# Scores of a query tile against high and low keys in one matmul

## The chip, the cores and the metric

The kernel runs on one core of a Trainium2 chip. The metric is the device time of one execution in microseconds; lower is better. TensorE multiplies matrices into the eight banks of PSUM; VectorE, ScalarE and GpSimd work on what lies in the banks (the first two only) and in SBUF; SyncE issues the loads of the weights. The engines run side by side and wait for one another only through semaphores.

## The reference

Two layers of a small decoder over 256 positions of width 1024, each a residual around one input projection, a mixer and one output projection. What the change touches is the attention inside both mixers. The even layer has 8 heads of causal attention over the one block of 256 keys:

```python
l_own = jnp.einsum('bhqd,bhkd->bhqk', qc, k_own).astype(jnp.float32) * scale
l_own = jnp.where((kpos[None, :] <= qpos[:, None])[None, None], l_own, -jnp.inf)
p = jax.nn.softmax(jnp.concatenate([l_sel, l_own], axis=-1), axis=-1)
```

The odd layer has 16 heads, each with three windows of strides 1, 4 and 16, merged with weights in proportion to their denominators. With 256 positions this is one softmax over masked scores, with a key that lies in two or three windows counted so often; the kernel puts the logarithm of the count in the mask. So both layers need, for each head, scores = q k^T plus a mask, then the exponential, the sum and the product with the values.

## The kernel before, in words

Everything in float32 that goes through TensorE as a projection or as scores is split in two parts, high (rounded to a shorter format, fp32r) and low (what is left), and the product is the sum of high x high, high x low and low x high. Weights come by DMA into `w_raw`; ScalarE rounds them to `w_hi` (L631), VectorE subtracts to get `w_lo` (L780), and TensorE runs three matmuls a piece (L1011, L1013, L1015 with 256 columns; L1052 to L1054 with 512).

The work of all engines follows one list made by `steps()`: a hundred "product" items on TensorE, and between them, at places written out by hand (`HEADS_AT`, `EVEN_AT`, `NORM_AT` and so on), the steps of the heads. Each engine walks this list and does its own part of every step, so the order within an engine is fixed and waits are only on semaphores.

A head goes through four steps. "scores": TensorE writes q k^T to one of two banks (`score_banks[n % 2]`), VectorE adds the mask, scales and writes to `probs`, keeping the least value for each query (`least`), and ScalarE takes the exponential and its sum. "divide": VectorE. "transpose": TensorE turns `probs`, ScalarE copies to SBUF. "values": TensorE, for four heads at once.

The heads are worked in three sets of 8: set 0 the even layer's, sets 1 and 2 the odd layer's. For each head the queries stand as high and low parts stacked over the 128 rows (`q_stack`), and the high key stands twice (`k_twice`), so that one matmul gives (high + low of q) x high key. The low key (`k_low`) has zeros in the other half, so a second matmul adds high q x low key. Query tile 0 (positions 0 to 127) needs keys 0 to 127 only; tile 1 needs all 256. That is four matmuls a head: columns 0 to 127 of the bank twice (L1071, L1072), columns 128 to 383 twice. Columns 384 to 511 are not used.

VectorE's step (L924) is one instruction per query tile, of 128 and 256 columns, each followed by a read of its accumulator; the second signals `masked`. ScalarE waits for `masked` of the head, and TensorE's scores of head n wait for `masked` of head n - 2 (the bank). TensorE's transpose of head n waits for the division of head n (L932) and for ScalarE's copy of head n - 1. In the even layer VectorE also does the layer norm between the heads (L876 to L884), with a reciprocal root on GpSimd. `yT_lo` serves as the twice-written key in sets 0 and 1, and `k_own` in set 2.

Of the kernel before, what the change touches and what calls it, by code (L numbers as in the profile page):

```python
# [20 lines left out]
P = 128  # L21
SEQ = 256
# [224 lines left out]
def build(nc, x, x_turned, final_norm_g, ab_w_in, ab_w_out, gmlp_ln_g, gmlp_ln_b, gmlp_w_s, gmlp_b_s,  # L247
# [12 lines left out]
    with ctx:  # L260
# [3 lines left out]
        def sem(name):  # L264
            return ctx.enter_context(nc.semaphore(name))
# [8 lines left out]
        hnT_hi = sb("hnT_hi", [P, CHUNKS, SEQ], fp32r)  # L274
        hnT_lo = sb("hnT_lo", [P, CHUNKS, SEQ], fp32r)
        yT_hi = sb("yT_hi", [P, CHUNKS, SEQ], fp32r)
        yT_lo = sb("yT_lo", [P, CHUNKS, SEQ], fp32r)
        q_own = sb("q_own", [P, HEADS_OF_SET, SEQ], fp32r)
        k_own = sb("k_own", [P, HEADS_OF_SET, SEQ], fp32r)
        k_low = sb("k_low", [P, HEADS_OF_SET, SEQ], fp32r)  # L280
        v = sb("v", [P, TILES, D])
        gate = sb("gate", [P, 2, TILES, BLOCK])
        y = sb("y", [P, TILES, D])
# [18 lines left out]
        moments = sb("moments", [P, TILES, nc.vector.BN_STATS_DIM])  # L302
        meanvar = sb("meanvar", [P, TILES, nc.vector.BN_AGGR_DIM])

        ones = v[:, 0, 0:P]
        gain = gate[:, 0, :, :].rearrange("p a b -> p (a b)")
        xT = y[:].rearrange("p t c -> p (t c)").rearrange("p (k s) -> p k s", s=SEQ)
# [6 lines left out]

        q_stack = (yT_hi, yT_hi, q_own)
        k_twice = (yT_lo, yT_lo, k_own)

        ln_g, ln_b = gate[:, 0, 0, :], gate[:, 0, 1, :]

# [40 lines left out]
        added, scaled = sem("added"), sem("scaled")  # L360
        hidden_turned, hidden_hi, hidden_ready = sem("hidden_turned"), sem("hidden_hi"), sem("hidden_ready")
        scores_done, masked, probs_ready = sem("scores_done"), sem("masked"), sem("probs_ready")
        probs_turned, probsT_ready = sem("probs_turned"), sem("probsT_ready")
        values_done, inverted, attended = sem("values_done"), sem("inverted"), sem("attended")
        squared, inner_ready = sem("squared"), sem("inner_ready")
# [355 lines left out]
        def _(dve):  # L721
# [52 lines left out]
            for step in order:  # L774
# [98 lines left out]
                elif what == "layer_norm":  # L873
                    vt = hn[:, n, BLOCK:D]
                    dve.wait_ge(dve_emptied, dve_emptied_before(3) + 1)
                    chain(nc.vector.bn_stats(moments[:, n, :], vt), stats, n + 1)  # L876
                    nc.vector.bn_aggr(meanvar[:, n, :], moments[:, n, :]).then_inc(stats2, 1)
                    dve.wait_ge(stats2, n + 1)
                    dve.wait_ge(ln_loaded, 32)
                    nc.vector.scalar_tensor_tensor(out=vt, in0=vt, scalar=meanvar[:, n, 0:1], in1=ln_g,  # L880
                                                   op0=ALU.subtract, op1=ALU.mult).then_inc(centred, 1)
                    dve.wait_ge(centred, n + 1)
                    dve.wait_ge(ln_plus, 2 * n + 2)
                    nc.vector.scalar_tensor_tensor(out=vt, in0=vt, scalar=rstd[:, 6 + n:7 + n], in1=ln_b,  # L884
                                                   op0=ALU.mult, op1=ALU.add).then_inc(v_normed, 1)
                elif what == "mix_u":

                    dve.wait_ge(mix_done, n + 1)
                    dve.wait_ge(bias_loaded, 16)
                    dve.wait_ge(dve_emptied, dve_emptied_before(5) + 1)  # L890
                    for g in range(GROUPS):
                        cols = slice(g * P, (g + 1) * P)
                        last = nc.vector.scalar_tensor_tensor(
                            out=y[:, n, cols], in0=score_banks[n][:, cols], scalar=bias_s[:, g:g + 1],
                            in1=hn[:, n, cols], op0=ALU.add, op1=ALU.mult)
                    last.then_inc(mixed, 1)
                elif what == "gating":
                    for t in range(TILES):
                        if n == 1:

                            dve.wait_ge(mixed, TILES)
                            dve.wait_ge(dve_emptied, dve_emptied_before(6) + 1)
                            last = nc.vector.scalar_tensor_tensor(
                                out=y[:, t, 0:BLOCK], in0=y[:, t, 0:BLOCK], scalar=quarter_rstd2[:, t:t + 1],
                                in1=gate[:, 0, t, :], op0=ALU.mult, op1=ALU.mult)
                        else:
                            c = {0: 1, 2: 0, 3: 1}[n]
                            dve.wait_ge(attended, {0: EVEN_HEADS, 2: EVEN_HEADS + 8, 3: N_HEADS}[n] // BATCH)
                            dve.wait_ge(dve_emptied, dve_emptied_before({0: 4, 2: 15, 3: 16}[n]) + 1)
                            part = y[:, t, BLOCK:D] if n == 0 else y[:, c, t * BLOCK:(t + 1) * BLOCK]  # L910
                            last = nc.vector.tensor_tensor(part, part, gate[:, c, t, :], ALU.mult)
                    last.then_inc(gated, 1)
                elif what == "scores":

                    mask = mask_even if n < EVEN_HEADS else mask_odd
                    dve.wait_ge(scores_done, n + 1)
                    if n == 0:
                        dve.wait_ge(const_pool, 2)
                    if n == EVEN_HEADS:
                        dve.wait_ge(mask_built, 2)  # L920
                    if n >= 3:
                        dve.wait_ge(probs_turned, n - 2)
                    for t, (a, b) in enumerate(((0, P), (P, 3 * P))):
                        last = nc.vector.tensor_tensor_reduce(  # L924
                            out=probs[:, n % 3, a:b], in0=score_banks[n % 2][:, a:b], in1=mask[:, 2 * P - (b - a):],
                            scale=-SCALE, scalar=3e38, op0=ALU.add, op1=ALU.min, accum_out=least[:, n, t:t + 1])
                    last.then_inc(masked, 1)
                elif what == "divide":
                    dve.wait_ge(probs_ready, n + 1)
                    chain(nc.vector.reciprocal(den[:, n, :], den[:, n, :]), inverted, n + 1)  # L930
                    for t, (a, b) in enumerate(((0, P), (P, 3 * P))):
                        last = nc.vector.tensor_scalar(probs[:, n % 3, a:b], probs[:, n % 3, a:b], den[:, n, t:t + 1],  # L932
                                                       None, ALU.mult)
                    last.then_inc(probs_scaled, 1)
                elif what == "values":
                    dve.wait_ge(values_done, n + 1)
                    nc.vector.tensor_copy(turned_y(n), value_bank[:]).then_inc(attended, 1)
                elif what == "y_pair":
                    chunk, bank = y_place(n)
                    dve.wait_ge(y_hi, n + 1)  # L940
                    source = bank[:] if n in GMLP_PAIRS else turned_y(n if n < 2 else n - 2)
                    nc.vector.tensor_tensor(yT_lo[:, chunk:chunk + 2, :], source.rearrange("p (a b) -> p a b", b=SEQ),
                                            yT_hi[:, chunk:chunk + 2, :].bitcast(fp32), ALU.subtract).then_inc(y_lo, 1)
                elif what == "residual":
                    layer, t, c = n // TILES, n % TILES, step[2]
                    group = (7, 17)[layer] + t

                    dve.wait_ge(products_done, LAST_ITEM_OF_GROUP[group] + 1 - 2 * (1 - c))
                    cols = slice(c * BLOCK, (c + 1) * BLOCK)
                    nc.vector.tensor_tensor(h[:, t, cols], h[:, t, cols], pair(group)[c][:],  # L950
                                            ALU.add).then_inc(added, 1)
                elif what == "windows":
                    windows()
                elif what == "scale":
                    dve.wait_ge(added, 2 * n + 2)
                    scale_tile(2 + n, 2 if n < TILES else 1)
                elif what == "hidden":
                    hidden_low(n)

        @block.tensor  # L960
        def _(pe):
# [15 lines left out]
            for step in order:  # L977
# [79 lines left out]
                elif what == "scores":  # L1057
# [8 lines left out]
                        pe.wait_ge(masked, n - 1)  # L1066
                    q, k = q_stack[heads_set], k_twice[heads_set]
                    bank = score_banks[n % 2]
                    for t, (a, b) in enumerate(((0, P), (P, 3 * P))):
                        queries, keys = slice(t * P, (t + 1) * P), slice(0, b - a)  # L1070
                        nc.tensor.matmul(bank[:, a:b], q[:, i, queries], k[:, i, keys], start=True, stop=False)  # L1071
                        last = nc.tensor.matmul(bank[:, a:b], q[:, i, queries], k_low[:, i, keys],  # L1072
                                                start=False, stop=True)
                    last.then_inc(scores_done, 1)
                elif what == "transpose":
                    pe.wait_ge(probs_scaled, n + 1)
                    if n >= 1:
# [80 lines left out]
```

## Time and profile before

| | before |
|---|---|
| time, median of 3 runs | 264.58 us (264.01 to 265.3) |
| span of the profiled execution, first to last instruction | 261.6 us |
| TensorE matmul busy | 251.8 us, 96% |
| VectorE busy | 192.2 us, 73% |
| ScalarE busy | 159.2 us, 61% |
| GpSimd busy | 25.0 us, 10% |
| DMA | 44.59 MB, mean 170 GB/s |
| granted TensorE clock, mean | 0.997 of full speed |

The profiled execution's span is 3.0 us shorter than the median time; what lies around the span belongs to the execution but not to the program's instructions. A matmul's duration contains its way through the array, so matmuls overlap in the trace and their durations don't add up to time: the distance from one start to the next does. The same holds in part for VectorE, where an instruction often starts a little before the last one ends.

### The profile page before, as it was taken

The page shows a single profiled execution, that of the slowest core. Times are in us where ns is not written, and L with a number is a line of the kernel's source. Part 1 is how long each engine was busy: PE and PEld are TensorE (multiplying, and loading weights), DVE is VectorE, ACT ScalarE, POOL GpSimd, SP SyncE. Part 2 cuts the span into 40 slices and gives each one's busy share as a digit, 9 for nine tenths or more (in the row PEclk, how much of TensorE's full clock was granted, in tenths as well). Part 3 has the DMA queues.
Part 4 walks back from the last instruction along what each step waited for, and adds up shares of the span by engine and source line. Part 5 has one row for each costly group of instructions (what it writes and reads, how often), then busy time and mean ns, then how long its engine had stood idle before and what let it go on. Part 6 is the DMA issues. An engine that isn't in the chain of part 4 may idle for free.

```text
span 261.6 us, 4450 instructions
## 1 busy us (share of the span) xinstructions
PE 251.8 (96%) x1670; PEld 225.8 (86%) x1670; DVE 192.2 (73%) x383; ACT 159.2 (61%) x301; POOL 25.0 (10%) x52
## 2 busy tenths in 40 slices
PE   7999998999999999999999999999999999999990
PEld 6789997899888788887888999989999999987870
DVE  2977999988896999749577609396986779763643
ACT  5867776765737953746377646558688576550232
POOL 3007130001010000010200000210003000100021
PEclk9999999999999999999999999999999999999998
DMA  7999869350446466534638950827072440200004
GB/s 230 391 393 332 303 245 332 150 163 0 163 160 201 160 236 208 183 140 162 189 132 300 336 169 13 304 71 257 4 214 110 163 148 15 78 3 3 0 1 160
DMA packets 22452, 44.59 MB, mean 170 GB/s; under 512 B 1056, under 2 KB 1312, under 8 KB 22432
## 3 DMA queue, kind: packets, MB, share of 16 engines
q1 hardware_dynamic: 21712, 43.00, 47.8%
q10 hardware_dynamic: 576, 0.79, 0.9%
q0 software_dynamic: 144, 0.52, 0.6%
q8 instruction: 13, 0.21, 0.3%
q14 instruction: 7, 0.06, 0.1%
HBM read 43.26 MB, written 1.05 MB: 169 GB/s over the span
## 4 chain that ended last, share of the span: by engine, by line
PE 77%; DVE 9%; DMA 7%; issue 2%; ACT 2%; SPq 1%; POOLq 0%; POOL 0%; DVEq 0%
PE products L1052 12%; PE products L1054 12%; PE products L1053 12%; PE products L1011 10%; PE products L1015 10%; PE products L1013 10%; DMA w_raw<-in_ab_w_in 7%; DVE w_lo L780 4%; PE turned L963 4%; PE attended L1094 3%; DVE k_low L826 3%; PE scores L1071 2%; PE scores L1072 2%; DVE tanh L803 1%; ACT w_hi L631 1%
## 5 line engine op out<-in xcount | busy, mean ns | idle before, releaser
L780 DVE TENSOR_TENSOR w_lo<-w_raw,w_hi 128x1024 fp32r<-128x1024 f32 x74 | 88.9, 1226 | 7.3 <-ACT w_hi L631 6.6
L631 ACT CAST w_hi<-w_raw 128x1024 fp32r<-128x1024 f32 x74 | 75.6, 1047 | 26.3 <-PE products L1015 10.4
L1011 PE MATMUL products<-hnT_hi,w_hi 128*128 128x256 f32 x288 | 82.5, 286 | 0.3 <-DVE w_lo L780 0.3
L1015 PE MATMUL products<-hnT_hi,w_lo 128*128 128x256 f32 x288 | 81.5, 283 | 0.0
L1013 PE MATMUL products<-hnT_lo,w_hi 128*128 128x256 f32 x288 | 81.5, 283 | 0.0
L1011 PEld LDWEIGHTS products<-hnT_hi,w_hi 128*128 128x128 f32 x288 | 55.1, 191 | 0.9 <-DVE w_lo L780 0.7
L1013 PEld LDWEIGHTS products<-hnT_lo,w_hi 128*128 128x128 f32 x288 | 55.2, 192 | 0.0
L1015 PEld LDWEIGHTS products<-hnT_hi,w_lo 128*128 128x128 f32 x288 | 55.2, 192 | 0.0
L1052 PE MATMUL products<-w_hi,hnT_hi 128*128 128x512 f32 x80 | 31.9, 399 | 0.1
L687 ACT ACTIVATE probs<-probs,least 128x128 f32<-128x128 f32 (+1 forms) x48 | 21.4, 447 | 17.1 <-DVE least L924 17.1
L1054 PE MATMUL products<-w_lo,hnT_hi 128*128 128x512 f32 x80 | 31.2, 390 | 0.0
L1053 PE MATMUL products<-w_hi,hnT_lo 128*128 128x512 f32 x80 | 31.2, 390 | 0.0
L1052 PE MATMUL products<-w_hi,yT_hi 128*128 128x512 f32 x64 | 25.6, 400 | 0.0
L1053 PE MATMUL products<-w_hi,yT_lo 128*128 128x512 f32 x64 | 25.0, 390 | 0.0
L1054 PE MATMUL products<-w_lo,yT_hi 128*128 128x512 f32 x64 | 25.0, 390 | 0.0
L1052 PEld LDWEIGHTS products<-w_hi,hnT_hi 128*128 128x128 f32 x80 | 15.0, 188 | 3.4 <-issue 0.7
L1054 PEld LDWEIGHTS products<-w_lo,hnT_hi 128*128 128x128 f32 x80 | 15.0, 188 | 3.3
L1053 PEld LDWEIGHTS products<-w_hi,hnT_lo 128*128 128x128 f32 x80 | 15.1, 188 | 2.7
L1054 PEld LDWEIGHTS products<-w_lo,yT_hi 128*128 128x128 f32 x64 | 12.0, 188 | 2.6
L586 ACT ACTIVATE tanh<-h 128x512 f32<-128x512 f32 x8 | 5.1, 633 | 14.8 <-DVE h L950 14.7
L1052 PEld LDWEIGHTS products<-w_hi,yT_hi 128*128 128x128 f32 x64 | 12.0, 188 | 2.3 <-issue 0.2
L1053 PEld LDWEIGHTS products<-w_hi,yT_lo 128*128 128x128 f32 x64 | 12.0, 188 | 2.2
(152 smaller groups left out, 334.2 us busy)
## 6 DMA issues: line engine op xcount, KB each, us to landing
w_raw<-in_c_w_in SPq DMA_DIRECT2D x16, 1024.0 KB, 5.4
w_raw<-in_ab_w_in SPq DMA_DIRECT2D x12, 1024.0 KB, 6.1
w_raw<-in_ab_w_out SPq DMA_DIRECT2D x4, 1024.0 KB, 4.9
w_raw<-in_c_w_out SPq DMA_DIRECT2D x4, 1024.0 KB, 5.0
w_raw<-in_ab_w_in SPq DMA_DIRECT2D x4, 256.0 KB, 4.4
w_raw<-in_ab_w_in SPq DMA_DIRECT2D x2, 512.0 KB, 7.6
h<-in_x SPq DMA_DIRECT2D x2, 512.0 KB, 11.4
out<-hn SPq DMA_DIRECT2D x4, 256.0 KB, 2.2
```

Of the source, the lines that this page charges most:

```text
L631: nc.scalar.copy(w_hi[:, n % SPLIT_SLOTS, :, :], w_raw[:, half % RAW_SLOTS, part, :]).then_inc(hi_ready, 1)
L687: last = nc.scalar.activation(probs[:, n % 3, a:b], probs[:, n % 3, a:b], ACT.Exp, scale=-1.0, bias=least[:, n, t:t + 1], accum_out=den[:, ...
L780: nc.vector.tensor_tensor(w_lo[:, n % SPLIT_SLOTS, :, :], w_raw[:, half % RAW_SLOTS, part, :], w_hi[:, n % SPLIT_SLOTS, :, :].bitcast(fp32 ...
L826: last = nc.vector.tensor_tensor(to, bank[rows, :].rearrange("p (a b) -> p a b", b=SEQ), high.bitcast(fp32), ALU.subtract)
L963: return nc.tensor.matmul(to, of, ident[:], is_transpose=True, start=True, stop=True)
L1011: nc.tensor.matmul(to, wh, hi[:, chunk, :], start=begins and c % 2 == 0, stop=False, skip_group_check=True)
L1013: nc.tensor.matmul(to, wh, lo[:, chunk, :], start=False, stop=False, skip_group_check=True)
L1015: last = nc.tensor.matmul(to, wl, hi[:, chunk, :], start=False, stop=ends, skip_group_check=True)
L1052: nc.tensor.matmul(to[:], xh, w_hi[:, slot, half_item, :], start=begins, stop=False)
L1053: nc.tensor.matmul(to[:], xl, w_hi[:, slot, half_item, :], start=False, stop=False)
L1054: last = nc.tensor.matmul(to[:], xh, w_lo[:, slot, half_item, :], start=False, stop=ends)
L1094: last = nc.tensor.matmul(value_bank[rows_of(a), two * SEQ:(two + 1) * SEQ][:, queries], v[:, tile, column:column + HEAD], turned_probs(he ...
```

## The change

For query tile 0 one matmul of 256 columns takes the place of two of 128. Its moving operand is the high keys 0 to 127 and the low keys 0 to 127 of the head, which lie in neighbouring blocks of one tensor, `k_parts`, that takes the place of `yT_lo`, `k_low` and `k_own`. Its results go to the first and the last 128 columns of the bank and aren't summed there. VectorE first adds the last 128 columns and the mask into `probs`, then masks tile 1, waits for its own addition (`low_masked`) and masks tile 0 with the sum in the mask's place. Tile 1 on TensorE is as before. In sets 0 and 1 the high part goes to the front of the bank and the low one to the end, in set 2 the other way round.

```diff
-        yT_lo = sb("yT_lo", [P, CHUNKS, SEQ], fp32r)
         q_own = sb("q_own", [P, HEADS_OF_SET, SEQ], fp32r)
-        k_own = sb("k_own", [P, HEADS_OF_SET, SEQ], fp32r)
-        k_low = sb("k_low", [P, HEADS_OF_SET, SEQ], fp32r)
+        k_parts = sb("k_parts", [P, 3, HEADS_OF_SET, SEQ], fp32r)
...
+        yT_lo, k_low, k_own = (k_parts[:, i, :, :] for i in range(3))
...
+        k_both = (k_parts[:, 0:2, :, :], k_parts[:, 0:2, :, :], k_parts[:, 1:3, :, :])
...
-                    for t, (a, b) in enumerate(((0, P), (P, 3 * P))):
+                    bank = score_banks[n % 2]
+                    own_low = probs[:, n % 3, 0:P]
+                    nc.vector.tensor_tensor(own_low, bank[:, 3 * P:], mask[:, P:], ALU.add).then_inc(low_masked, 1)
+                    for t, (a, b) in ((1, (P, 3 * P)), (0, (0, P))):
+                        if t == 0:
+                            dve.wait_ge(low_masked, n + 1)
                         last = nc.vector.tensor_tensor_reduce(
-                            out=probs[:, n % 3, a:b], in0=score_banks[n % 2][:, a:b], in1=mask[:, 2 * P - (b - a):],
+                            out=probs[:, n % 3, a:b], in0=bank[:, a:b], in1=mask[:] if t else own_low,
                             scale=-SCALE, scalar=3e38, op0=ALU.add, op1=ALU.min, accum_out=least[:, n, t:t + 1])
                     last.then_inc(masked, 1)
...
-                    for t, (a, b) in enumerate(((0, P), (P, 3 * P))):
-                        queries, keys = slice(t * P, (t + 1) * P), slice(0, b - a)
-                        nc.tensor.matmul(bank[:, a:b], q[:, i, queries], k[:, i, keys], start=True, stop=False)
-                        last = nc.tensor.matmul(bank[:, a:b], q[:, i, queries], k_low[:, i, keys],
-                                                start=False, stop=True)
-                    last.then_inc(scores_done, 1)
+
+                    apart = bank[:].rearrange("p (a b) -> p a b", b=P)[:, 0:4:3, :]
+                    nc.tensor.matmul(apart, q[:, i, 0:P], k_both[heads_set][:, :, i, 0:P], start=True, stop=True)
+                    nc.tensor.matmul(bank[:, P:3 * P], q[:, i, P:SEQ], k[:, i, :], start=True, stop=False)
+                    nc.tensor.matmul(bank[:, P:3 * P], q[:, i, P:SEQ], k_low[:, i, :], start=False,
+                                     stop=True).then_inc(scores_done, 1)
```

## Rows read from the trace of the kernel before

**Rows 1.** The page: span, part 1 (busy) and part 4 (chain that ended last).

```profile
span 261.6 us, 4450 instructions
PE 251.8 (96%) x1670; PEld 225.8 (86%) x1670; DVE 192.2 (73%) x383; ACT 159.2 (61%) x301; POOL 25.0 (10%) x52
PE 77%; DVE 9%; DMA 7%; issue 2%; ACT 2%; SPq 1%; POOLq 0%; POOL 0%; DVEq 0%
```

**Rows 2.** TensorE's waits: releaser, us in total, times, longest us.

```profile
PE scores L1071 <- DVE least L924: 0.6, 1, 0.6
PE products L1011 <- DVE w_lo L780: 0.3, 1, 0.3
```

**Rows 3.** Busy time by stretch: length, each engine's busy us, clock, DMA share, GB/s.

```profile
171.00:233.00 62.00, 61.41 (x516) 58.93 (x516) 50.34 (x145) 42.32 (x104) 3.29 (x6) 1.00 0.34 111
```

**Rows 4.** TensorE's timeline around head 2: start us, duration us, line, operation, form.

```profile
47.60 0.39 PE L1054 MATMUL products<-w_lo,hnT_hi 128*128 128x512 f32 x1
47.82 0.22 PE L1071 MATMUL scores<-yT_lo,yT_hi 128*128 128x128 f32 x1
...
48.28 0.40 PE L1052 MATMUL products<-w_hi,hnT_hi 128*128 128x512 f32 x1
```

**Rows 5.** Timeline of the weight loads of head 12.

```profile
186.37 0.19 PEld L1071 LDWEIGHTS scores<-yT_lo,yT_hi 128*128 128x128 f32 x1
186.48 0.19 PEld L1072 LDWEIGHTS scores<-k_low,yT_hi 128*128 128x128 f32 x1
186.59 0.19 PEld L1071 LDWEIGHTS scores<-yT_lo,yT_hi 128*128 128x128 f32 x1
186.70 0.19 PEld L1072 LDWEIGHTS scores<-k_low,yT_hi 128*128 128x128 f32 x1
186.82 0.19 PEld L1011 LDWEIGHTS products<-hnT_hi,w_hi 128*128 128x128 f32 x1
```

**Rows 6.** TensorE's timeline: products of 256 columns, two in a row.

```profile
175.20 0.28 PE L1015 MATMUL products<-hnT_hi,w_lo 128*128 128x256 f32 x1
175.32 0.28 PE L1011 MATMUL products<-hnT_hi,w_hi 128*128 128x256 f32 x1
```

**Rows 7.** Groups by line and form: busy us, mean ns of one, idle before.

```profile
L924 DVE CUSTOM_DVE_ANT_0 probs<-scores,mask_odd 128x128 f32<-128x128 f32 x16 | 4.6, 286 | 0.8 <-PE scores L1072 0.7
L768 DVE SCALAR_TENSOR_TENSOR hnT_lo<-scores,gain_of,hnT_hi 128x128 fp32r<-128x128 f32 x8 | 2.2, 343 | 0.6 <-ACT hnT_hi L595 0.6
```

**Rows 8.** VectorE's timeline: the query splits and mask 0.

```profile
43.93 2.80 DVE L826 TENSOR_TENSOR yT_hi<-tanh,yT_hi 64x512 fp32r<-64x512 f32 x4
46.76 0.29 DVE L924 CUSTOM_DVE_ANT_0 probs<-scores,mask_even 128x128 f32<-128x128 f32 x1
...
46.98 0.42 DVE L924 CUSTOM_DVE_ANT_0 probs<-scores,mask_even 128x256 f32<-128x256 f32 x1
47.32 0.08 DVE L924 DVE_READ_ACCUMULATOR2_ANT least<- 128x1 f32 x1
```

**Rows 9.** TensorE's timeline: the transpose of head 3.

```profile
63.79 0.49 PE L963 MATMUL turned<-ident,probs 128*128 128x128 f32 x3
```

**Rows 10.** VectorE's timeline: mask 3, and the division of head 3.

```profile
58.30 0.29 DVE L924 CUSTOM_DVE_ANT_0 probs<-scores,mask_even 128x128 f32<-128x128 f32 x1 [0.41 <-PE scores L1072]
...
62.77 0.55 DVE L932 TENSOR_SCALAR probs<-probs,den 128x128 f32<-128x128 f32 x2
```

**Rows 11.** VectorE's timeline: the weight splits ahead of mask 8, and its end.

```profile
171.32 2.36 DVE L780 TENSOR_TENSOR w_lo<-w_raw,w_hi 128x1024 fp32r<-128x1024 f32 x2
...
174.27 0.08 DVE L924 DVE_READ_ACCUMULATOR2_ANT least<- 128x1 f32 x1
```

**Rows 12.** TensorE's timeline: the scores of head 10.

```profile
174.41 0.33 PE L1071 MATMUL scores<-yT_lo,yT_hi 128*128 128x128 f32 x1 [0.58 <-DVE least L924]
```

**Rows 13.** VectorE's timeline: the division of head 13.

```profile
194.96 0.55 DVE L932 TENSOR_SCALAR probs<-probs,den 128x128 f32<-128x128 f32 x2
```

**Rows 14.** TensorE's timeline: the transpose of head 13.

```profile
196.33 0.49 PE L963 MATMUL turned<-ident,probs 128*128 128x128 f32 x3
```

More of the change, by code:

```diff
@@ L362, in build @@
         scores_done, masked, probs_ready = sem("scores_done"), sem("masked"), sem("probs_ready")
+        low_masked = sem("low_masked")
         probs_turned, probsT_ready = sem("probs_turned"), sem("probsT_ready")
```

## The prediction

> **What bounds the kernel now.** I read the page first. TensorE is busy 96% of the span and carries 77% of the chain that ended last, VectorE 9% of it [rows 1]. A busy TensorE is not yet a bound, so the waits of TensorE come next: in the whole run it stands still on VectorE's score work for 0.6 us, in one place, and on the low halves of the weights for 0.3 us [rows 2]. The rest is matmuls back to back. So a microsecond taken from TensorE's stream comes off the span, unless VectorE is then late; and VectorE work costs nothing except at those places where TensorE reaches a wait soon after VectorE has signalled. VectorE has room on average: in the stretch with the odd layer's heads it is busy 50.34 of 62.00 us [rows 3]. The question is therefore local: what a head's matmuls cost, and where a later mask is felt.
>
> **What a head costs TensorE, and what is saved.** A head is four matmuls, each with its own weight load: 128 columns high and low for query tile 0, 256 columns high and low for tile 1. Start to start from the first of them to the next product, head 2 takes 48.28 - 47.82 = 0.46 us [rows 4]. The weight loads show why: they start 0.11, 0.11, 0.11 and 0.12 us apart, whatever the width of the matmul behind them [rows 5]. A matmul of 128 columns thus takes a turn of 0.11 us, one of 256 columns 0.12 us, which the products of 256 columns confirm (0.12 us from one to the next, each with a load) [rows 6]. The change leaves three matmuls of 256 columns: 3 x 0.12 = 0.36 us. It saves 0.46 - 0.36 = 0.10 us a head, 24 x 0.10 = 2.4 us in all. The number of columns stays 768 a head, so this gain exists only because a turn is bounded by its load and not by its columns.
>
> The new matmul reads its moving operand in two pieces of 128 columns, 2048 elements apart (8 heads x 256: high and low keys lie in neighbouring blocks of one tensor), and writes 128 columns at either end of a bank. The trace has no matmul of this form. Below, it can't beat a load's turn, 0.11 us; above, I bound it by a product of 512 columns, 0.22 to 0.23 us (47.60 to 47.82) [rows 4]. I take 0.12, the row of the same width, as the columns, the partitions and the bank are the same.
>
> A rule speaks against the change. The Trainium skill (TensorE: Matmul & The Clock Gate, "Back-to-back issue gap") gives an isolated gap of N/2.4 + 2.5 ns; by that a head would be about 330 ns before and 328 ns after, and the change would save nothing. The measured 0.46 us a head disagrees with it here. A rival below has the same outcome, worked out from rows.
>
> **What VectorE gets.** Each head gains one addition of 128 x 128 from a bank and SBUF to SBUF, and the two masks swap places. The mask of 128 columns lasts 286 ns [rows 7] and that of 256 columns 0.42 us [rows 8], but the next instruction starts before it ends: 46.76 to 46.98 is 0.22 us for the first, 46.98 to 47.32 is 0.34 us for the second [rows 8]. The addition isn't in the trace. Nearest are the mask of the same shape (0.22 us to the next) and the scaled subtraction of 128 x 128 from a bank, 343 ns long (some 0.27 us to the next if it overlaps as the masks do) [rows 7]. I take 0.21 to 0.22 us: like the mask it has no pointer operand. The floor is the time of its 128 elements by the difference of the two masks, about 0.13 us; the ceiling the whole 0.34 us. The wait for the addition's own semaphore (low_masked) is set in front of the last mask, with a mask of 0.34 us between; the semaphore has long risen, so I cost the wait at nothing, and at up to 0.04 us if that cover were gone. Behind it on VectorE stand the next splits and divisions, and ScalarE's exponentials wait for the same masked signal. Total 24 x 0.21 = 5 us of VectorE.
>
> The Trainium skill (VectorE: DVE Perf Modes, "The DRAIN you can't avoid") says that the next instruction doesn't start until the pipe is empty, by which an addition would hold VectorE for its full length. The starts above contradict it by 0.08 us; by the page the four additions that I charge below would cost 0.3 us more.
>
> SBUF gets the same bytes under another name, the GpSimd clearing and key copies work on the same elements, no DMA is added or moved, and no queue is passed. Those cost nothing.
>
> **Where the addition reaches the path.** I went through every wait of TensorE on a mask, on a division (the transposes) and on ScalarE's copy, and compared it with the end of what it waits for. Three are tight.
>
> *Scores of head 2* wait for mask 0. VectorE comes to mask 0 when its query splits end (43.93 + 2.80 = 46.73) [rows 8], not when the scores do, so mask 0 ends 0.21 us later: 47.40 becomes 47.61. TensorE comes at 47.82 - 2 x 0.10 = 47.62, but its weight load, which carries the wait, wants to go about 0.1 us ahead. So of the 0.20 us gained about 0.15 is lost, and 0.05 stays; with head 2 itself the lead is 0.15.
>
> *Transpose of head 3*, at 63.79 [rows 9]. Its division ends at 62.77 + 0.55 = 63.32 [rows 10], 0.47 us before. That division comes out of a chain which starts when the scores of head 3 are done: mask 3 at 58.30, mask 4, the layer norm's statistics, a trip over GpSimd, and the division [rows 10]. Two additions are now inside it, 0.42 us, while its start comes 0.15 + 0.10 = 0.25 earlier. The division ends at 63.32 + 0.42 - 0.25 = 63.49 and TensorE can go at about 63.65 (signal and load, as above). TensorE's lead there is 0.14 us, in place of the 0.55 (7 x 0.10 - 0.15) that heads 0 to 6 would give: 0.4 us lost. With head 7 the lead is 0.24 at the end of the even set. Up to head 8 all further work, the norm and the splits of the keys, is led by TensorE and keeps this lead.
>
> *Scores of head 10* wait for mask 8; this is the 0.6 us wait [rows 2]. VectorE is in one run from the key splits over two weight splits (171.32 + 2.36 = 173.68) to mask 8, whose last part ends at 174.35, and TensorE starts at 174.41 [rows 11, 12]. Here 0.21 us of addition goes straight on the path, and what heads 8 and 9 save turns into longer waiting. Lead: 0.24 - 0.21 = 0.03.
>
> From head 10 on, heads 10 to 23 save 14 x 0.10 = 1.4 us. The tightest division left with a mask ahead of it is that of head 13, which ends at 194.96 + 0.55 = 195.51, 0.8 us before its transpose at 196.33 [rows 13, 14]; additions and TensorE's lead together take at most 0.5 us of that. The division of head 16 is tighter still, but follows a copy of TensorE's own output with no mask between, so it keeps step. The low halves of weights are several microseconds ahead (how seldom they are waited for: [rows 2]).
>
> **Sum:** 0.03 + 1.4 = 1.43, and some 0.05 more for turns of 0.113 and not 0.11: 1.5 us. The profiled execution is 261.6 us from first to last instruction, and 3.0 us lie around it up to the median of 264.58; the change doesn't touch those. 264.58 - 1.5 = 263.1 us.
>
> **The rivals.**
> (a) *TensorE's time goes by columns, and the change doesn't do what it says.* No gain; mask 8 adds 0.21, and transpose 3 about 0.1: 264.9 us. Against it: at the rate of the 512-column product (0.23 us) 768 columns would take 0.34 us, and a head takes 0.46. 0.07.
> (b) *The two-piece matmul is slow.* One mechanism, at L1071's replacement: the additions alone cost about 0.3 us (mask 8 and the transpose of head 3, as in (a)), which heads 10 to 23 earn with 0.02 us each, so it decides from 0.12 + 0.08 = 0.20 us on; at the bound of 0.23 us a head takes 0.47 us, 24 x 0.01 = 0.2 us are lost instead of saved, and with the additions' 0.3 us the time is 265.1 us, slower than before. For it: no row shows the form. Against it: a stride within a partition's row is nothing that the low and high halves don't have already. 0.10.
> (c) *The additions hold VectorE for 0.34 us.* Then four of them on the path cost 0.13 us more each, 0.5 us: 263.6 us. For it: the length of the scaled subtraction. 0.15.
> (d) *The additions hide.* VectorE's order lets mask 0 and the division of head 3 come in time, and only mask 8 counts: 22 x 0.10 - 0.21 = 2.0 us, or 2.4 us if not even that: 262.4 us. Against it: the three tight places. 0.15.
> The forecast has the remaining 0.53.
>
> **Numbers.** Predicted 263.1. Low end: case (d) with the turns at 0.113, 262.2. High end: between (c) and (a), with the spread of the runs shown (264.01 to 265.3), 264.4. Leaving out (a), (b) and the lowest part of (d) leaves out two in ten. A measurement of this kernel can tell 0.5% from no change, that is 1.3 us: 263.26 is the border, and the forecast lies just beyond it. Faster: most of (d) and two thirds of the forecast, 0.5. Slower by over 0.5% needs 265.9, which (b) reaches only if the matmul is worse than its bound: 0.05. The rest, 0.45, within.
>
> **What the profile after would show.** A head of 0.36 us start to start; three loads; the addition at 0.29 us with the next instruction 0.21 us after its start; a wait for mask 8 grown from 0.6 to about 1.0 us; a short wait of TensorE at the transpose of head 3; and the last product 1.4 to 1.5 us earlier. What would make it wrong: a two-piece matmul that isn't 0.12 us, an addition of over 0.3 us to the next, or a fourth tight place that VectorE's shifted queue makes.

## The result, and the profile after

The changed kernel takes 261.82 us (median of six executions, 261.52 to 262.04), the kernel before 264.29 us (median of six beside it, 263.68 to 265.56). The ratio is 0.9915, 95% interval 0.9891 to 0.9939: faster by 0.85%, between 0.61% and 1.09%. The forecast was 263.1 us with a range from 262.2 to 264.4: the direction was right, and the time lies 0.4 us below the range.

The page of the changed kernel: span, busy time and, after the dots, the chain that ended last.

```profile
span 260.3 us, 4426 instructions
PE 249.4 (96%) x1646; PEld 223.3 (86%) x1646; DVE 196.4 (75%) x407; ACT 158.9 (61%) x301; POOL 25.0 (10%) x52
...
PE 75%; DVE 11%; DMA 7%; issue 2%; ACT 2%; SPq 1%; POOL 1%; POOLq 0%; DVEq 0%
```

Beside [rows 1]: TensorE has 24 instructions less and VectorE 24 more, one for each head. VectorE's share of the chain grew from 9 to 11%. A span also holds the first loads, whose arrival differs between executions, so I compare the part behind them: from the first scores matmul to the last product. In the kernel before these two stand at 45.46 and 254.72, 209.26 us apart; in the changed one they are these, 207.68 us apart.

```profile
45.78 0.36 PE L1078 MATMUL scores<-k_parts,yT_hi 128*128 128x256 f32 x1 [1.10 <-DVE yT_hi L828]
...
253.46 0.39 PE L1061 MATMUL products<-w_lo,yT_hi 128*128 128x512 f32 x1
```

That is 1.58 us less, where the sum was 1.4 to 1.5. Below, "the stream" is the same stretch up to the start of the third matmul from the end, where the last half item of products begins. It is 208.80 us in the kernel before (208.81 in a second trace of it, below) and 207.23 us in the changed one: 1.57 us less. Each of the two kernels has two traces; in these it repeats to 0.01 and 0.07 us, where whole times of one kernel differ by up to 2 us. One profiled execution below, that of the semaphore alone, took 418.87 us at a granted clock of 0.56 and gives no stream.

Head 1 on TensorE's timeline (start us, duration us, line, operation, form):

```profile
46.21 0.28 PE L1078 MATMUL scores<-k_parts,yT_hi 128*128 128x256 f32 x1
46.33 0.28 PE L1079 MATMUL scores<-k_parts,yT_hi 128*128 128x256 f32 x1
46.45 0.28 PE L1080 MATMUL scores<-k_parts,yT_hi 128*128 128x256 f32 x1
46.56 0.40 PE L1059 MATMUL products<-w_hi,hnT_hi 128*128 128x512 f32 x1
```

From first matmul to next product a head takes 46.56 - 46.21 = 0.35 us, where head 2 took 0.46 [rows 4]. The first of the three is the matmul with the moving operand in two pieces and its result at both ends of the bank; its turn is 0.12 us like that of the others. The weight loads of head 12 say the same, beside [rows 5]:

```profile
186.34 0.19 PEld L1078 LDWEIGHTS scores<-k_parts,yT_hi 128*128 128x128 f32 x1
186.45 0.19 PEld L1079 LDWEIGHTS scores<-k_parts,yT_hi 128*128 128x128 f32 x1
186.57 0.19 PEld L1080 LDWEIGHTS scores<-k_parts,yT_hi 128*128 128x128 f32 x1
186.69 0.19 PEld L1018 LDWEIGHTS products<-hnT_hi,w_hi 128*128 128x128 f32 x1
```

VectorE's timeline at mask 0, beside [rows 8]. The first row is the addition: 0.20 us to the next instruction. The last mask, which waits for low_masked, starts 0.34 us after the mask of 256 columns, and 0.34 us is also what follows that mask in the kernel before, where nothing waits (46.98 to 47.32).

```profile
47.08 0.30 DVE L927 TENSOR_TENSOR probs<-scores,mask_even 128x128 f32<-128x128 f32 x1
47.28 0.42 DVE L931 CUSTOM_DVE_ANT_0 probs<-scores,mask_even 128x256 f32<-128x256 f32 x1
47.62 0.08 DVE L931 DVE_READ_ACCUMULATOR2_ANT least<- 128x1 f32 x1
47.62 0.29 DVE L931 CUSTOM_DVE_ANT_0 probs<-scores,probs 128x128 f32<-128x128 f32 x1
```

The stretch with the odd layer's heads, beside [rows 3]: VectorE is busy 53.33 us in place of 50.34, with 162 instructions in place of 145.

```profile
171.00:233.00 62.00, 61.01 (x507) 58.24 (x506) 53.33 (x162) 43.09 (x107) 3.26 (x6) 1.00 0.34 111
```

The three tight places. TensorE's wait for mask 8, at the scores of head 10 (releaser, us in total, times, longest), beside [rows 2]:

```profile
PE scores L1078 <- DVE least L931: 1.0, 1, 1.0
```

It is 1.0 us in place of 0.6. The two others are short gaps on the timeline, at the scores of head 2 and the transpose of head 3:

```profile
47.72 0.39 PE L1061 MATMUL products<-w_lo,hnT_hi 128*128 128x512 f32 x1
47.98 0.39 PE L1078 MATMUL scores<-k_parts,yT_hi 128*128 128x256 f32 x1
48.20 0.28 PE L1079 MATMUL scores<-k_parts,yT_hi 128*128 128x256 f32 x1
...
63.44 0.28 PE L1022 MATMUL products<-hnT_hi,w_lo 128*128 128x256 f32 x1
63.84 0.55 PE L970 MATMUL turned<-ident,probs 128*128 128x128 f32 x3
```

At head 2 the first matmul starts 0.26 us behind a product of 512 columns, where it was 0.22 [rows 4], and its own turn is 0.22 in place of 0.12: from product to scores 0.04 us is lost, and in the head 0.10, so the 0.10 that this head should save is gone and 0.04 more. At head 3 the transpose starts 0.40 us after a product whose turn is 0.12 us: 0.28 us lost. The rows of the weight loads at the two places name what they waited for, mask 0 and the division of head 3:

```profile
47.98 0.19 PEld L1078 LDWEIGHTS scores<-k_parts,yT_hi 128*128 128x128 f32 x1 [0.29 <-DVE least L931]
...
63.84 0.31 PEld L970 LDWEIGHTS turned<-ident,probs 128*128 128x128 f32 x3 [0.33 <-DVE probs L939]
```

### The profile page after: what moved, and what is told of

It is laid out like the page before. It is cut to its first block, busy times and chain, and to the rows that moved or that the text cites. A ratio compares the mean times of both kernels' runs of the same rounds, so it can differ in the third digit from the quotient of the medians.

```text
span 260.3 us, 4426 instructions
## 1 busy us (share of the span) xinstructions
PE 249.4 (96%) x1646; PEld 223.3 (86%) x1646; DVE 196.4 (75%) x407; ACT 158.9 (61%) x301; POOL 25.0 (10%) x52
## 4 chain that ended last, share of the span: by engine, by line
PE 75%; DVE 11%; DMA 7%; issue 2%; ACT 2%; SPq 1%; POOL 1%; POOLq 0%; DVEq 0%
PE products L1059 12%; PE products L1061 12%; PE products L1060 12%; PE products L1018 9%; PE products L1022 9%; PE products L1020 9%; DMA w_raw<-in_ab_w_in 7%; DVE w_lo L782 5%; PE turned L970 4%; PE attended L1101 3%; DVE k_parts L828 3%; PE scores L1078 1%; DVE tanh L805 1%; PE scores L1080 1%; PE scores L1079 1%
## 5 line engine op out<-in xcount | busy, mean ns | idle before, releaser
L1060 PE MATMUL products<-w_hi,k_parts 128*128 128x512 f32 x64 | 25.0, 390 | 0.0
L538 POOL CAST k_parts<-k_parts 64x512 fp32r<-64x512 f32 x12 | 8.5, 706 | 77.8 <-ACT k_parts L645 77.2
```

The source lines that it names most:

```text
L538: nc.gpsimd.tensor_copy(to[rows_of(1 - side), heads_of(i, side), :], to[rows_of(side), heads_of(i, side), :].bitcast(fp32)).then_inc(keys_ ...
L1060: nc.tensor.matmul(to[:], xl, w_hi[:, slot, half_item, :], start=False, stop=False)
```

## The experiments

Each ratio is against executions of the kernel before on the same chip, with its 95% interval. The times of several single edits can't be told from no change, so the reading goes by the stream of the profiled execution, and by the time less its own span, which each execution gives. The diffs of the addition alone, the matmul alone, the four heads and the two tight places are against the changed kernel, the last one against the version with the eased places, the others against the kernel before; "..." marks what is left out.

**The kernel before, unchanged.** Its edit is empty.

> The kernel before, unchanged. Two theories of why the change measured 2.5 us (0.85%) where the two profiled executions differ by 1.3 us (261.6 and 260.3): (A) the profiled execution of before was a quick one of a kernel whose executions spread, and the change's true worth is what TensorE's stream shows, 1.3 to 1.5 us, plus something that the slower executions of before lose at a place where the new kernel doesn't; then the spans here spread from 261.6 to over 263 us with 1.7 us around each, as in the new kernel, and the slow ones lose it in the first 45 us, where the loads of the weights set the pace. (B) before has 3.0 us around its span and the executions are alike; then the spans here lie within 0.5 us of 261.6.

263.77 us, ratio 1.0009 (0.9991 to 1.0027), beside 29 executions with a median of 263.70 (263.38 to 265.59). The stream is 208.81. Two findings. The time less the span is 2.01 to 2.10 us in all twelve, not 3.0. And the times bunch: 36 of these 41 between 263.4 and 264.1, five between 264.7 and 265.6. The profiled one took 264.67 us, span 262.6, and shows where such time goes. The third piece of x on which ScalarE works waits for its load:

```profile
8.70 0.51 ACT L604 ACTIVATE hnT_hi<-y,hn 128x256 fp32r<-128x256 f32 x1 [2.17 <-DMA y<-in_x_turned]
```

In the first trace of the same kernel the row of the same piece is this, without a wait:

```profile
6.72 0.51 ACT L604 ACTIVATE hnT_hi<-y,hn 128x256 fp32r<-128x256 f32 x1
```

The stream behind it is equal to 0.01 us. So the difference between these two arises before it, and the late load of x is what the trace shows there. Two other traces below are of long executions too: 262.92 us in the matmul alone (median 261.50) and 263.22 us in the four heads (median 261.92). In these ScalarE waits 0.75 and 0.82 us for its first piece of x, where the other traces have 0 to 0.6, and the first scores matmul starts at 46.95 and 47.24, against 46.50 in the one above and 45.30 to 46.07 in the traces of shorter executions. For the long executions without a trace the same cause is likely and not shown.

**The tensor alone.** `k_parts` in place of the three, all the rest as before.

> Only the three tensors yT_lo, k_low and k_own are put into k_parts; matmuls and masks as before. If the other addresses in SBUF are worth something (theory C), this is 0.5 to 1 us faster than before; by A and B it is the same, ratio within 0.2% of 1.

```diff
-        yT_lo = sb("yT_lo", [P, CHUNKS, SEQ], fp32r)
-        k_own = sb("k_own", [P, HEADS_OF_SET, SEQ], fp32r)
-        k_low = sb("k_low", [P, HEADS_OF_SET, SEQ], fp32r)
+        k_parts = sb("k_parts", [P, 3, HEADS_OF_SET, SEQ], fp32r)
...
+        yT_lo, k_low, k_own = (k_parts[:, i, :, :] for i in range(3))
```

263.79 us, 1.0003 (0.9987 to 1.0019), stream 208.82. The place of the keys costs nothing.

**The addition alone.** Four matmuls, the low one of tile 0 to the end of the bank; VectorE as in the changed kernel.

> Four matmuls as before, but the low one of tile 0 goes to the end of the bank, and VectorE adds and masks as in the new kernel. By the account of the tight places: mask 0 has 0.4 us of room, the division of head 3 0.4 and mask 8 none, so 0.2 us at mask 8 and up to 0.1 at the transpose of head 3: 0.2 to 0.4 us slower than before (0.1%). If the additions weigh more than I think (0.34 us each): 0.5 to 0.8 us slower.

```diff
-                    nc.tensor.matmul(apart, q[:, i, 0:P], k_both[heads_set][:, :, i, 0:P], start=True, stop=True)
+                    nc.tensor.matmul(bank[:, 0:P], q[:, i, 0:P], k[:, i, 0:P], start=True, stop=True)
+                    nc.tensor.matmul(bank[:, 3 * P:], q[:, i, 0:P], k_low[:, i, 0:P], start=True, stop=True)
```

263.71 us, 0.9992 (0.9975 to 1.0008), stream 209.07: 0.27 longer than before. Its wait for mask 8:

```profile
PE scores L1078 <- DVE least L931: 0.8, 1, 0.8
```

0.6 became 0.8: with TensorE's number of matmuls unchanged, 24 additions cost little more than one. From the scores of head 9 to those of head 10 it is 1.41 us (173.33 to 174.74) in place of 1.21 (173.20 to 174.41), which is 0.20 for the addition. The whole time did not follow the stream: the time less the span is 1.69 to 1.84 us here, against 2.01 to 2.10 in the kernel before.

**The matmul alone.** One matmul of 256 columns, no addition, VectorE as before. This kernel leaves the low keys out of tile 0's scores, so it computes something else and serves only for its time.

> The one matmul of 256 columns, without the addition: the low keys of tile 0 are left out of its scores, VectorE works as before. TensorE saves 24 x 0.10 = 2.4 us, less what heads 8 and 9 save (0.2) and a part of heads 0 and 1: 2.1 to 2.3 us against before by the stream, span near 259.4. If the measured gain of the new kernel holds 1 us of something else (theory C), 3.2 us.

```diff
-                    nc.vector.tensor_tensor(own_low, bank[:, 3 * P:], mask[:, P:], ALU.add).then_inc(low_masked, 1)
-                    for t, (a, b) in ((1, (P, 3 * P)), (0, (0, P))):
-                        if t == 0:
-                            dve.wait_ge(low_masked, n + 1)
+                    for t, (a, b) in enumerate(((0, P), (P, 3 * P))):
...
-                            out=probs[:, n % 3, a:b], in0=bank[:, a:b], in1=mask[:] if t else own_low,
+                            out=probs[:, n % 3, a:b], in0=bank[:, a:b], in1=mask[:, 2 * P - (b - a):],
```

261.50 us, 0.9905 (0.9875 to 0.9935), stream 206.61: 2.19 us less than before. The time less the span is 2.02 to 2.09, as in the kernel before. Its wait for mask 8:

```profile
PE scores L1075 <- DVE least L928: 0.8, 1, 0.8
```

Two heads of saving, 0.2 us, went into that wait, and the other 22 x 0.10 = 2.2 arrive. The two parts alone give -2.19 + 0.27 = -1.92, together they give -1.57. The remaining 0.35 us is their meeting: once TensorE is ahead, additions are felt that weren't at TensorE's old pace. Which ones, the experiment with four heads below tells.

**The changed kernel again.**

> The changed kernel, unchanged, beside the same runs of before as the next three. The executions of before fall in two groups, most near 263.7 us and some near 265.3 us, by how the first loads arrive, so that three or six of them give an uneven median. If the true gain is the stream's (span 261.6 to 260.1, 1.5 us) and 0.35 us around the span (2.07 before, 1.72 in the changed kernel), the two medians differ by 1.9 us, ratio 0.993. If the first measurement of 2.5 us holds, 0.9905.

262.01 us (261.76 to 263.20), 0.9935 (0.9913 to 0.9957), beside seventeen executions of the kernel before with a median of 263.74. Stream 207.30, time less span 1.67 to 1.76. Against this even sample of the kernel before, the change brings 263.74 - 262.01 = 1.7 us, 0.65%.

**Four heads in the old form.** Heads 0, 3, 4 and 8, whose additions I had charged, keep four matmuls and two masks.

> Heads 0, 3, 4 and 8, whose additions lie on the path by my account, are done as before (two matmuls of 128 columns, no addition), the other twenty as in the change. By the account: TensorE saves 19 x 0.10 (head 9's goes into the wait for mask 8), the wait for mask 8 is 0.2 us shorter than in the changed kernel and that at the transpose of head 3 goes: span 1.9 us under before, 0.3 to 0.4 us under the changed kernel. If additions cost by their number on VectorE and not by their place: TensorE loses 0.4 us, VectorE gains little, and it is 0 to 0.4 us slower than the changed kernel.

```diff
+AS_BEFORE = (0, 3, 4, 8)
...
+                    if n in AS_BEFORE:
+                        nc.tensor.matmul(bank[:, 0:P], q[:, i, 0:P], k[:, i, 0:P], start=True, stop=False)
+                        nc.tensor.matmul(bank[:, 0:P], q[:, i, 0:P], k_low[:, i, 0:P], start=False, stop=True)
+                    else:
+                        nc.tensor.matmul(apart, q[:, i, 0:P], k_both[heads_set][:, :, i, 0:P], start=True, stop=True)
```

261.92 us (261.24 to 263.22), 0.9927 (0.9902 to 0.9953). The times can't be told from those of the changed kernel; the stream can: 206.88, 0.35 less than 207.23. Its wait for mask 8:

```profile
PE scores L1085 <- DVE least L934: 0.7, 1, 0.7
```

Four heads gave back 0.1 us each of saving and the stream still became shorter. So these four additions cost 0.65 to 0.75 us between them (0.65 if head 8's saving is taken to go into the wait for mask 8 in any case, as in the matmul alone). The other twenty cost at most 0.2: their heads save 20 x 0.105 = 2.1 us, 0.2 more than the 1.92 measured.

**Two tight places eased by the order.** The changed kernel, with the transpose of head 3 and the scores of head 10 each one half item of products later in the order written out by hand.

> The changed kernel with two places moved: the scores of head 10 one half item later (behind a product, 1.44 us), and the transpose of head 3 one later. Then mask 8 (ends 174.5) is there before TensorE comes (174.9), and the division of head 3 too. By the account this takes off the waits of 1.15 and 0.3 us, and mask 9 may then be late by 0.1 to 0.3 for the scores of head 11: 1.1 to 1.4 us faster than the changed kernel, span near 258.9. If the waits come back in full elsewhere: the same as the changed kernel.

```diff
-     (6, 8, 10, 13, 18, 19, 21, 23),
+     (6, 8, 10, 14, 18, 19, 21, 23),
...
-     (3, 4, 4, 6, 11, 13, 13, 14)),
+     (3, 4, 5, 6, 11, 13, 13, 14)),
```

260.99 us (260.63 to 262.35), 0.9897 (0.9873 to 0.9921), stream 206.21, 1.02 us less than the changed kernel's. The wait for mask 8 is gone from TensorE's waits. This is the fastest of the kernels tried. The largest gap that remains is further on, at the transpose of head 8 and the scores of head 11, which now meet mask 9:

```profile
176.49 0.28 PE L1022 MATMUL products<-hnT_hi,w_lo 128*128 128x256 f32 x1
176.61 0.49 PE L970 MATMUL turned<-ident,probs 128*128 128x128 f32 x3
177.08 0.39 PE L1078 MATMUL scores<-k_parts,yT_hi 128*128 128x256 f32 x1
```

From transpose to scores it is 0.47 us, where head 12 needs 0.25 in the changed kernel (186.12 to 186.37): 0.2 us lost.

**The same places in the kernel before.** The two lines of the last diff, in the kernel before.

> The kernel before with the same two places. Its wait for mask 8 is 0.75 us and it has none at the transpose of head 3, so 0.6 to 0.75 us faster than before. The difference of e7 and this is then the change freed of the places where its additions are felt: 24 x 0.10 = 2.4 us, less at most 0.3.

263.03 us, 0.9975 (0.996 to 0.999), stream 207.96, 0.84 less than before; time less span 2.01 to 2.12. So most of the gain from the order is there without the change. With the order eased in both, the change is worth 207.96 - 206.21 = 1.75 us of stream and 263.03 - 260.99 = 2.0 us of time (0.33 of it around the span). I had expected 2.1 to 2.4 of stream: a miss. The gap at mask 9, 0.2 us, the scores of head 2, some 0.1, and a gap of 0.17 us ahead of the transpose of head 10 (184.94 to 185.23, where the turn is 0.12) make up most of the difference from 2.4.

**The semaphore alone.** In the kernel before, the first mask of each head also signals `low_masked`, for which nobody waits.

> The kernel before; the first mask of each head also signals low_masked, which nobody waits for. The time around the span is 2.0 to 2.1 us in before and in every kernel without the additions, and 1.7 to 1.8 us in every kernel with them. If one more semaphore in use makes the difference, it is 1.7 us here; if it goes by VectorE's number of instructions, 2.0 to 2.1 us. Span as before, 261.6 us.

```diff
+                        if t == 0:
+                            last.then_inc(low_masked, 1)
...
```

263.80 us, 1.0003 (0.9979 to 1.0026), time less span 2.01 to 2.11: as the kernel before. Neither the semaphore nor its signals move what lies around the span.

**Twenty-four more instructions on VectorE.** In the kernel before, one addition of one column a head, into a column of the bank that nothing reads.

> The kernel before with one more tiny VectorE instruction a head (one column, into a column of the bank that nobody reads) and no new semaphore. If the number of instructions makes the difference around the span, 1.7 to 1.8 us here; if the semaphore, 2.0 to 2.1 us. The span may grow by some 0.1 us, since the instruction stands ahead of mask 8.

```diff
+                    nc.vector.tensor_tensor(score_banks[n % 2][:, 3 * P:3 * P + 1], mask[:, 0:1], mask[:, 1:2], ALU.add)
```

263.46 us, 0.9988 (0.9975 to 1.0001), which as a whole time isn't clear of no change. The time less the span is 1.68 to 1.76 us, as in the changed kernel. Part 3 of the page (packets, MB, share) shows one thing that goes with it, here

```profile
q14 instruction: 8, 0.07, 0.1%
```

and in the kernel before

```profile
q14 instruction: 7, 0.06, 0.1%
```

The kernels with 7 packets (before, the tensor alone, the matmul alone, the places in the kernel before, the semaphore alone) have 2.01 to 2.12 us around the span, those with 8 (changed, the addition alone, the four heads, this one, the last one below) 1.67 to 1.84. The version with the eased places has 9 packets and 1.70 to 1.75, so one packet more changes nothing further. What the kernels of the second group have in common is 20 to 24 instructions more on VectorE, and an addition of one column does as well as one of 128. TensorE's number doesn't matter: the matmul alone has 24 less and 2.02 to 2.09. Why a longer program on VectorE should end or begin in less time outside the span, no run here shows.

**The places, head 0 in the old form, head 11 later.** From the version with the eased places.

> The changed kernel with the two places of e7, the scores of head 11 also one half item later (in e7 they wait some 0.2 us for mask 9), and head 0 done as before, so that mask 0 isn't late for the scores of head 2. By the account of the tight places: 0.2 to 0.4 us off e7 in the span from the first scores to the last product (206.2 us in e7): 205.8 to 206.0 us, and 1.1 to 1.4 us under the changed kernel. If moving a wait only moves it on, 206.2 us or more.

```diff
-     (3, 4, 5, 6, 11, 13, 13, 14)),
+     (3, 4, 5, 7, 11, 13, 13, 14)),
...
+AS_BEFORE = (0,)
...
```

261.40 us (261.30 to 262.94), 0.9927 (0.9908 to 0.9946), stream 206.95: 0.74 us worse than the version it came from, where 0.2 to 0.4 better was expected. ScalarE's timeline, then TensorE's:

```profile
180.46 0.40 ACT L690 ACTIVATE probs<-probs,least 128x128 f32<-128x128 f32 x1 [0.65 <-DVE least L934]
...
181.35 2.36 ACT L646 CAST q_own<-products 64x512 fp32r<-64x512 f32 x4
...
184.81 0.48 ACT L698 COPY probsT<-turned 128x384 f32<-128x384 f32 x1
```

```profile
185.43 0.52 PE L973 MATMUL turned<-ident,probs 128*128 128x128 f32 x3 [1.02 <-ACT probsT L698]
```

The exponential of head 11 comes later and ScalarE stands at it for its mask; behind it in ScalarE's order are the split of the queries and the copy of the turned `probs`, and TensorE waits 1.02 us for that copy at the transpose of head 10. The step that I moved had room on TensorE and on VectorE, and none on ScalarE. The two traces also show how far the expectation held. Counted from the first scores matmul, TensorE is 0.02 us ahead of the version with the eased places at the scores of head 8, so head 0 in the old form gives back about what it gains, and 0.26 us ahead at the transpose of head 9, so the later scores of head 11 did bring some 0.24. At the transpose of head 10 it is 0.75 us behind.

## Why the prediction was right or wrong

**What a head saves: right.** 0.35 us a head in place of 0.46. By the matmuls of head 1 the saving is 0.11 us, by the weight loads of head 12 it is 0.10; 24 x 0.105 = 2.5 us. Rival (a), time by columns, is out: the 768 columns of a head are what they were, and the head is a quarter shorter. By the formula in the Trainium skill (TensorE: Matmul & The Clock Gate, "Back-to-back issue gap") the estimate is 328 ns for the new head and 330 for the old; it comes near the 0.35 of three wide matmuls and misses the 0.46 with narrow ones, whose loads start 0.11 us apart. But the section itself calls this the gap of an isolated matmul and says that for narrow ones in a stream with weight loads it counts too little, so the prediction was wrong to call it a rule against the change.

**The two-piece matmul: right.** Taken at 0.12 from the row of the same width; it is 0.12. Rival (b) is out.

**The addition: right.** Taken at 0.21 to 0.22 to the next instruction, 0.20 to 0.21 measured, with a length of 285 ns at its line. The next instruction starts 0.08 us before it ends. The prediction took from the Trainium skill (VectorE: DVE Perf Modes, "The DRAIN you can't avoid") that it would wait for the end. The same section adds that a next instruction which isn't held starts earlier, and with that the trace agrees. The wait for `low_masked` costs nothing. Rival (c), 0.34 us, is out.

**The tight places: right, with small errors.** The wait for mask 8 went from 0.6 to 1.0 us, as forecast. The transpose of head 3 waits. The lead of TensorE lost there is 0.28 us, where I had 0.4; the loss at the scores of head 2 is 0.14, where I had 0.15. The wait for mask 8 is 0.4 longer. Together 0.82 us, of 2.5 - 1.57 = 0.95 that is lost of the heads' saving. Of the 0.4 at mask 8, 0.2 is the saving of heads 8 and 9, which goes into that wait without any addition too (the matmul alone). The other 0.6 is the additions', and the four heads in the old form show that it is nearly all due to the four that I had charged. Rival (d), in which the additions hide, is out, though the time came out near its 262.4. The time alone would have pointed to the wrong mechanism.

**The sum of the stream: right.** -1.43 to -1.5 forecast, -1.57 in one trace and -1.50 in another.

**The step that failed** is the one that turns the stream into a time: "The profiled execution is 261.6 us from first to last instruction, and 3.0 us lie around it up to the median of 264.58; the change doesn't touch those." Both halves are wrong. The 3.0 was the span of one execution taken from the median of others. In every execution of this kernel where span and time are both known 2.0 to 2.1 us lie around the span, so the profiled one probably took about 263.7 us, which is none of the three shown (the lowest is 264.01), and their median was 0.9 above it. That "probably" rests on the constancy of the 2.0 to 2.1, for the profiled execution's own time isn't known. And the change does touch it: 2.05 became 1.72. With both put right, 264.58 - 0.9 - 0.33 - 1.5 = 261.85, and 261.82 was measured.

**The range.** Its ends held the unknown costs of matmul and addition and the spread of single executions upwards, but nothing for where in that spread the three shown lay. With three values that cover 1.3 us, their median could itself be wrong by most of 1 us in either direction, and the range should have gone to about 261.3.

**The border of 0.5%.** The first comparison has a median of before that lies 0.5 us above that of the larger samples, so its 0.85% is high; 0.65% (0.43% to 0.87%) is the better figure. Both say faster, and about a fifth of that is the 0.33 us around the span, which 24 additions of one column brought too.

## What to carry to other kernels

Take a time's base from a span and a total of the same execution, and where only a median of few runs is shown, put their spread into both ends of the range. Where matmuls with a load each are narrow (here a turn of 0.11 us at 128 columns and 0.12 us at 256), count loads and not columns, and fold two narrow ones into a wide one. Before work is added to another engine, list TensorE's waits with the slack of each: a few places carry the whole cost, the lead that the saving gives makes slack vanish at others, and before a step is moved the order of every engine that takes part in it must be read, ScalarE's too.

## What the runs showed of the hardware that wasn't expected

- A matmul of 256 columns that reads two blocks of 128 columns 2048 elements apart and writes both ends of a bank takes the turn of a plain one, 0.12 us.
- Around the span lie 2.01 to 2.12 us in kernels with VectorE's instructions as before, 1.67 to 1.84 us in those with 20 to 24 more; a queue of instruction loads has 8 or 9 packets in place of 7 there. The cause is open.
- Executions of one kernel differ by up to 2 us. Two traced ones of the kernel before differ by 1.0 us of span with a stream equal to 0.01 us; in the longer one ScalarE waited 2.17 us for a load of x for which it didn't wait in the other.
